# Attention stage turned round: keys on the partitions instead of queries

## The reference, cut to what matters

```python
# 8 heads, q: 1024 queries of 96 numbers, k: 1280 keys (1024 + 256), v: 64 numbers a key
def one(qi):                                   # a block of 128 queries
    s = einsum('bqhd,bkhd->bhqk', qi, k) * 96 ** -0.5
    p = softmax(s, axis=-1)                    # over the 1280 keys
    return einsum('bhqk,bkhd->bqhd', p, v)
...
yd = attn * silu(d_gate)                       # then into the output product
```

## Time and profile before

| what | value |
|---|---|
| runs, median (lowest to highest) | 3601.41 us (3597.78 to 3604.99) |
| the profiled execution's own time | 3603.62 us |
| its span | 3601.8 us |
| busy share of the span: PE, PEld | 91%, 84% |
| DVE, ACT, POOL | 56%, 26%, 6% |
| attention loop in the span | from 3015.8 to 3414.0 us |

### The profile page before, as it was taken

One profiled execution on the slowest core, in us unless ns is written; L12 is line 12 of the kernel. 1 busy time (PEld: TensorE's weight loads), 2 busy tenths in 40 slices (PEclk: granted clock), 3 DMA queues, 4 the chain that ended last, 5 costly groups with the idle time before them and its releaser, 6 DMA issues. The chain is left out here.

```text
span 3601.8 us, 47693 instructions
## 1 busy us (share of the span) xinstructions
PE 3289.2 (91%) x20158; PEld 3042.2 (84%) x20158; DVE 2008.2 (56%) x2814; ACT 943.8 (26%) x1178; POOL 227.4 (6%) x224
## 2 busy tenths in 40 slices
PE   3999999999688779999999999899988996988887
PEld 3999999999677679999999999899988983555465
DVE  5565655566568444566446446645445535666446
ACT  3222222222323331121111111221133314444323
POOL 0000000000005200000000000000012000222200
PEclk9999999999798789999999999999989997999898
DMA  3222222222343344321321321411121321000031
GB/s 100 91 78 75 90 85 86 90 89 74 137 102 50 95 170 135 129 77 53 106 81 46 108 79 38 153 37 43 50 74 37 128 87 74 1 1 1 22 133 69
DMA packets 102463, 285.76 MB, mean 79 GB/s; under 512 B 13157, under 2 KB 32101, under 8 KB 101993
## 3 DMA queue, kind: packets, MB, share of 16 engines
q1 hardware_dynamic: 102248, 282.70, 24.6%
HBM read 218.68 MB, written 63.98 MB: 78 GB/s over the span
## 5 line engine op out<-in xcount | busy, mean ns | idle before, releaser
L491 PE MATMUL mixer_in_dense<-mix_z_high,mixer_in_whigh 128*128 128x348 f32 x1344 | 445.8, 332 | 11.3 <-POOL mixer_in_out L328 11.3
L491 PE MATMUL mixer_in_dense<-mix_z_high,mixer_in_wlow 128*128 128x348 f32 x1344 | 439.1, 327 | 0.0
L491 PE MATMUL mixer_in_dense<-mix_z_low,mixer_in_whigh 128*128 128x348 f32 x1344 | 438.2, 326 | 0.0
L1372 PE MATMUL flow_dense<-rst_norms_operand_b_high,flow_whigh 128*128 128x342 f32 x1248 | 399.2, 320 | 0.4 <-DVE flow_wlow L1464 0.4
L1372 PE MATMUL flow_dense<-irst_norms_operand_b_low,flow_whigh 128*128 128x342 f32 x1248 | 398.3, 319 | 0.0
L1372 PE MATMUL flow_dense<-rst_norms_operand_b_high,flow_wlow 128*128 128x342 f32 x1248 | 397.4, 318 | 0.0
L1930 PE MATMUL joint_dense<-rst_norms_operand_b_high,joint_whigh 128*128 128x342 f32 (+2 forms) x1056 | 344.7, 326 | 17.0 <-DVEq L2047 10.1
L1930 PE MATMUL joint_dense<-rst_norms_operand_b_high,joint_wlow 128*128 128x342 f32 (+2 forms) x1056 | 341.7, 324 | 0.0
L1930 PE MATMUL joint_dense<-irst_norms_operand_b_low,joint_whigh 128*128 128x342 f32 (+2 forms) x1056 | 340.6, 323 | 0.0
L1372 PE MATMUL flow_dense<-first_operand_a_high,flow_whigh 128*128 128x342 f32 (+1 forms) x912 | 291.4, 320 | 26.9 <-DVEq L1485 26.9
L1372 PE MATMUL flow_dense<-first_operand_a_low,flow_whigh 128*128 128x342 f32 (+1 forms) x912 | 291.8, 320 | 0.0
(11 more groups left out here) (544 smaller groups left out, 6201.3 us busy)
## 6 DMA issues: line engine op xcount, KB each, us to landing
mixer_in_wstage<-w_in SPq DMA_DIRECT2D x56, 512.0 KB, 4.6
mixer_in_mod_w<-w_mod SPq DMA_DIRECT2D x64, 384.0 KB, 3.6
first_norms_weights<-w_up SPq DMA_DIRECT2D x44, 512.0 KB, 3.5
flow_side<-h SPq DMA_DIRECT2D x24, 512.0 KB, 4.3
h<-flow_out SPq DMA_DIRECT2D x24, 512.0 KB, 3.2
first_norms_weights<-ab_w_in SPq DMA_DIRECT2D x20, 512.0 KB, 3.6
p<-mixer_in_out SPq DMA_DIRECT2D x16, 528.0 KB, 2.9
first_norms_weights<-w_down SPq DMA_DIRECT2D x16, 512.0 KB, 3.5
```

Source lines behind the costliest of these rows:

```text
L491: mm = pe.matmul(pd[s % 2][:, 0:W], a[n % 2][:, P * m:P * (m + 1)], z[x][:, m, W * b:W * (b + 1)], start=m == 0 and i == 0, stop=m == DT - ...
L1372: mm = pe.matmul(o, w[n % NW][:, P * k:P * (k + 1)], x[h][:, k, where], start=k == 0 and e == 0, stop=k == kt - 1 and e == 2)
```

## The change

Each half of a head (512 queries) becomes one unit, 16 in all, with the keys on the partitions:

- `peak`: for each of four tiles of 128 queries one pass of high*high over the 1280 keys, into 3 PSUM banks (one buffer); DVE `largest` takes the maxima. These belong to the next unit.
- `rows`: PE turns the four columns of maxima into a row of 512, negated (product with -identity), ACT `row` copies it as a 97th row of the queries; the keys get a 97th row of ones. So the score product itself subtracts the maximum.
- `chunk`: ten times the whole product for 128 keys x 512 queries (three matmuls of 512 columns) into a ring of three PSUM banks; ACT takes exp of it straight into the buffer from which `value_sums` reads. No transposes, no moves.
- sums over keys: POOL `add_keys` adds the ten blocks (5 blocks to 5, then 2 to 2, 1 to 1, 1 to 1), PE `key_sums` multiplies with ones, DVE `finish` takes 1/sum of 64 x 512, multiplies it with the gate, adds the two halves of the values product, and multiplies.
- For the last unit DVE does `add_keys`.

The order within a unit is written out in `unit`; DVE's program for unit U begins with `finish(U-2)`.

```diff
+    def made_at(U):
+        h, b = divmod(U, 2)
+        if h + 1 >= NH:
+            return (), (), ()
+        if b:
+            return (), (("q", h + 1, 1),), ()
+        return (("k", h + 1, 0),), (("k", h + 1, 1), ("k", h + 1, 2)), (("q", h + 1, 0),)
+
+    def unit(U):
+        own = [[("e", U, k)] for k in range(NKT)]
+        first_, second_, third_ = made_at(U)
+        if U == 0:
+            for k in range(NKT):
+                own[k].append(("v", k))
+        if U + 1 < UNITS:
+            for q, k in enumerate((1, 3, 5, 7)):
+                own[k].append(("peak", U + 1, q))
+            own[6].append(("rows", U + 1, 0))
+        if U:
+            for p, k in enumerate((2, 3, 5, 7)):
+                own[k].append(("sums", U - 1, p))
+        own[2] += first_
+        own[4] += second_
+        own[8] += third_
+        if U + 1 < UNITS:
+            own[9].append(("rows", U + 1, 1))
+        if U:
+            own[9] += [("keys", U - 1), ("sums", U - 1, 4)]
+        return [n for k in own for n in k]
...
+        def add_keys(ch, tt, U):
+            p = PT[U % 2]
+            ch.do(tt(acc[:, :, :], p[:, 0:5, :], p[:, 5:10, :], ALU.add))
+            ch.do(tt(acc[:, 0:2, :], acc[:, 0:2, :], acc[:, 2:4, :], ALU.add))
+            ch.do(tt(acc[:, 0, :], acc[:, 0, :], acc[:, 1, :], ALU.add))
+            ch.do(tt(acc[:, 0, :], acc[:, 0, :], acc[:, 4, :], ALU.add))
...
+                def peak(U, q):
...
+                    if i:
+                        pe.wait_ge(maxed, i)
+                    q0 = HALF * b + P * q
+                    for k0, w in ((0, 512), (512, 512), (1024, 256)):
+                        mm = pe.matmul(pS[:, k0:k0 + w], qh[h % 2][0:KD, q0:q0 + P], kh[h % 2][0:KD, k0:k0 + w],
+                                       start=True, stop=True, skip_group_check=True)
+                    mm.then_inc(peaked, 1)
+
+                def rows(U, r):
...
+                    for q in (2 * r, 2 * r + 1):
+                        i = 4 * U + q
+                        pe.wait_ge(maxed, i + 1)
+                        mm = pe.matmul(pR[:, P * q:P * q + P], mx[:, i:i + 1], minus[:, :], start=True, stop=True,
                                        skip_group_check=True)
...
+                def chunk(n):
...
+                    if k == 0:
+                        pe.wait_ge(lows, HL.at(h, f"rope{b}"))
...
+                        pe.wait_ge(rows_in, U + 1)
                     o = wait_free(pe, n)
+                    pe.matmul(o, kh[j][0:KD + 1, keys], qh[j][0:KD + 1, at], start=True, stop=False)
+                    pe.matmul(o, kl[j][0:KD, keys], qh[j][0:KD, at], start=False, stop=False)
+                    pe.matmul(o, kh[j][0:KD, keys], ql[j][0:KD, at], start=False, stop=True).then_inc(full, 1)
+
+                def value_sums(U, p):
+                    h = U // 2
+                    if p == 0:
+                        if U == 0:
+                            pe.wait_ge(v_made, 1)
+                        else:
+                            pe.wait_ge(y_added, U)
+                        pe.wait_ge(exped, NKT * (U + 1))
...
+                def key_sums(U):
+                    pe.wait_ge(added, U + 1)
+                    if U:
+                        pe.wait_ge(inverted, U)
+                    pe.matmul(pK, c["ones"][:, 0:VD], acc[:, 0, :], start=True, stop=True).then_inc(keys_full, 1)
...
+                def row(U):
+                    act.wait_ge(rows_full, U + 1)
+                    act.activation(qh[U // 2 % 2][KD:KD + 1, half_of(U)], pR, ACT.Copy).then_inc(rows_in, 1)
...
+                            act.activation(PT[U % 2][:, k, :], pt[ring[n] % RING], ACT.Exp, scale=scale).then_inc(exped, 1)
...
+                def largest(U, q):
+                    i = 4 * U + q
+                    dve.wait_ge(peaked, i + 1)
+                    dve.tensor_reduce(mx[:, i:i + 1], pS[:, 0:T2], AX.X, ALU.max).then_inc(maxed, 1)
+
+                def finish(U):
+                    h, at, own = U // 2, half_of(U), rows_of(U)
+                    dve.wait_ge(keys_full, U + 1)
+                    ch.do(dve.reciprocal(ri[own, :], pK))
+                    dve.sem_inc(inverted, 1)
+                    if U == 0:
+                        dve.wait_ge(gates_in, 64)
+                    ch.inc(tt(ri[own, :], ri[own, :], dg[own, h // 2, at], ALU.mult))
+                    dve.wait_ge(y_moved, U + 1)
+                    if h >= 2:
+                        dve.wait_ge(y_low, 2 * (h // 2 - 1) + U % 2 + 1)
+                    ch.do(tt(yp[own, at], pY[own, :], ytmp[own, :], ALU.add))
+                    dve.sem_inc(y_added, 1)
+                    ch.do(tt(yp[own, at], yp[own, at], ri[own, :], ALU.mult))
+                    dve.sem_inc(y_ready, 1)
...
+                ch = Chain(pool, pstep)
+                for U in range(UNITS - 1):
+                    pool.wait_ge(exped, NKT * (U + 1))
+                    if U:
+                        pool.wait_ge(keys_full, U)
+                    add_keys(ch, pool.tensor_tensor, U)
+                    pool.sem_inc(added, 1)
```

More of the change, by code:

```diff
@@ L2399, in attend @@
+    first = tuple(("k", 0, b) for b in range(3)) + tuple(("q", 0, b) for b in range(2))
+    program = [unit(U) for U in range(UNITS)]
+    names = first + tuple(n for own in program for n in own if n[0] in "ekqv")
+    ring = Places(names)
+    by_act = ring.count([n for n in names if n[0] == "v" and n[1] % 2 == 0])
+    by_dve = ring.count([n for n in names if n[0] in "kqv" and n not in by_act])
     with Phase(nc, "attn") as ph:
@@ L2490, in pair_scores @@
[L2490 to L2499, removed]
-                    o = wait_free(pe, n)
[L2501 to L2527, removed]
+                            pe.wait_ge(ones_in, 2)
@@ L2541, in _ @@
                     make(n)
[L2542 to L2547, removed]
-                            make(n)
[L2549 to L2558, removed]
+                for q in range(4):
+                    peak(0, q)
@@ new lines, in _ @@
+                rows(0, 0)
+                rows(0, 1)
+                for U in range(UNITS):
+                    for n in program[U]:
+                        if n[0] == "e":
+                            chunk(n)
+                        elif n[0] == "peak":
+                            peak(n[1], n[2])
+                        elif n[0] == "rows":
+                            rows(n[1], n[2])
+                        elif n[0] == "sums":
+                            value_sums(n[1], n[2])
+                        elif n[0] == "keys":
+                            key_sums(n[1])
+                        else:
+                            make(n)
@@ L2560, in _ @@
+                for p in range(4):
+                    value_sums(UNITS - 1, p)
+                key_sums(UNITS - 1)
+                value_sums(UNITS - 1, 4)
             @block.scalar
             def _(act):
[L2562 to L2573, removed]
@@ new lines, in _ @@
+                dve.wait_ge(step, ch.n)
+                for q in range(4):
+                    largest(0, q)
+                for U in range(UNITS + 2):
+                    if U == UNITS:
+                        dve.wait_ge(exped, NKT * UNITS)
+                        dve.wait_ge(keys_full, UNITS - 1)
+                        add_keys(ch, tt, UNITS - 1)
+                        dve.sem_inc(added, 1)
+                    if U >= 2:
+                        finish(U - 2)
+                    if U >= UNITS:
+                        y_rest(U - 2)
+                        continue
+                    for n in program[U]:
+                        if n[0] == "peak":
+                            largest(n[1], n[2])
+                            if n[2] == 2 and U >= 2:
+                                y_rest(U - 2)
+                        elif n[0] == "v":
+                            if n not in by_act:
+                                dve.wait_ge(full, ring[n] + 1)
+                                dve.tensor_copy(V[:, n[1], :], pt[ring[n] % RING]).then_inc(dve_freed, 1)
+                                if n[1] == NKT - 1:
+                                    dve.wait_ge(act_freed, by_act[("v", NKT - 2)])
+                                    dve.wait_ge(dve_freed, by_dve[n])
+                                    dve.sem_inc(v_made, 1)
+                        elif n[0] in "kq":
+                            low(n)
+                    if U == UNITS - 1:
+                        y_rest(U - 2)
```

236 lines of the change are left out of this document (92 added, 144 removed).

## The result

The changed kernel took 3675.87 us (median of 4 runs, 3672.19 to 3678.55); the kernel before, run beside it, 3599.6. The ratio is 1.0216, interval 1.0203 to 1.0229: slower by some 76 us, where 3592 was forecast and 3632 was the end of the range. The profiled execution took 3672.19 us with a span of 3670.0. Every median here is over undisturbed executions: one of the kernel before, beside the last two experiments, took 4802 us at a clock of 0.64 and is left out.

A forecast was written before the change was run, and what follows sets the result against it. The prediction took the loop as bound by its chain of waits, not one engine. The ends' -26.8 us plus 17.6 for the clock gave -9.2: 3592 against the median 3601.4 (3594 for the profiled execution); range 3560 to 3632.

The forecast's parts named there:

- what PE needs: PE's work: 15.2 of 22.84 us per half head in the old loop, 13.7 us per unit after the change.
- The walk: Step-by-step timing of DVE, PE and ACT through one unit from chunk 0: periods 22.9 and 22.3, mean 22.6 us.
- the hold: In `finish`, POOL's first and second additions delay DVE's two-SBUF-input products: gate product done at 5.75, last product at 8.7 us.
- The reciprocal is hidden: In `finish`, DVE's 3.34 us reciprocal runs beside POOL's first addition; up to 5.3 us for it costs nothing.
- The clock's term: Granted clock falls in most units' thin PE stretch: 1.2 us a unit, 15.6 for 13 units, plus 2 in the tail.
- the signs that the prediction named: Reciprocals 3.3 us, products far over 0.69, PE's wait about 3.9 us, period 22.6 to 24, clock near 0.85, among others.
- The ends: Start, first and last units and tail: the stage ends at 3387.2 instead of 3414.0 without the clock, 26.8 us less.
- Rival 5: Loop: more small waits missing from the walk, 2 us a unit and up, with the clock; 3640 and above; chance 0.05.
- Rival 2: Loop: PE stays at 1.2 GHz through second and third peak of every unit, 3 us x 13; 3616; chance 0.27.
- Rival 3: `finish`: DVE and POOL do not hold each other, saving 38 us and 15 of clock cost; 3540; chance 0.06.

The follow-up runs named there:

- reordered kernel: Changed kernel with DVE doing halves' sum, first maximum, reciprocal, second and third maximum, then the two products; ACT's upper-half copy moved from exponential 5 to 8: 3576.77 us.
- experiment 3: Changed kernel with 14 small float32 matmuls as fillers, results unread, put on PE just before its wait for `y_added`: 3659.42 us, ratio 1.0167.
- the eighth experiment: Reordered kernel with reciprocal and both products together right after the first maximum, and ACT's copy back at exponential 5: 3624.72 us, ratio 1.0091.
- experiment 4: Changed kernel with four of the ten values products of a unit left out, one from each of four pairs: 3673.57 us, ratio 1.0205.

## Why the prediction was wrong

**The step that failed: what PE needs.** "A pair of values products 0.43 (four take 1.08, two at a time); a float32 matmul of 512 columns 0.43 (eight take 3.70)". The counts are of records, two to a float32 matmul: four are one pair, 1.0 us, and eight in 3.70 are four matmuls (their records start 0.43 apart, 3218.70 to 3220.41), 0.86 us each. (The Trainium skill, "FP8 and Floating Point Precision", "TensorE Precision Notes", says that true FP32 takes 4 passes through the array. The trace agrees: four times the 0.23 us of one score matmul is 0.92, near the 0.86 to 1.0 measured.) The sum for a unit then is 13.7 + 5 x 0.57 for the pairs + 1.1 for q and k (1.31 for half of q and half of k's 0.95 + 1.43, 2.5 against 1.4) + 0.43 for the key sum = 18.1. `rows` takes 2 x 0.53 for 0.45, and some seven chunks and four peaks 0.1 to 0.2 more next to float32 work: about 2 more, 20. The reordered kernel shows 20.6.

I had a check and talked it away. The earlier trace rows had PE busy for 271.80 of 300 us, 20.7 of 22.84 a half head, and the prediction said that it "overstates" this, as matmuls overlap. It hardly did. By it PE had 2 us of slack in a period, not 7.6; and the change's work, as the reordered kernel does it, is 20.6. The change takes **nothing** off PE: the transposes that go are paid for by peaks and rows.

**What followed.** The walk was right to the first maximum and wrong behind it. From chunk 0 of the unit above at 3213.71:
- `y_added` at 6.3 (6.5 forecast), PE's stall 3.45 (3.85), last product done 8.4 (8.7), first maximum done 10.05 (10.25). Gate product and last product took 2.52 and 2.01 here (2.43 and 1.80 in the mean), as the hold asked.
- second maximum done at 13.07 (12.45 forecast), q full at 16.2 (13.0), third maximum done 21.6 (18.4), fourth 24.0 (20.65), end of the unit 27.4 (22.3). The 3.2 us that come in by q are the pair, q's own matmuls and a chunk, dearer than thought and in part at 0.50; the last 1.8 are a `rows`, a pair and the key sum.

In other words, with 20.6 us of work, PE can afford neither a stall nor a low clock. By the window of the changed kernel PE is idle for (300 - 253.18) / 300 x 28.6 = 4.5 us of a unit and busy for 24.1, of which 20.6 is the work as the reordered kernel does it at a clock of 0.99; the other 3.5 come with the clock at 0.87. That is 20.6 + 4.5 + 3.5 = 28.6, where the forecast had 13.7 of work and waits of DVE and PE on each other to fill up to 22.6, and 1.2 for the clock. "The reciprocal is hidden" was true of `y_added` and false of the unit.

**Right:** reciprocal 3.35 us (3.34), POOL's first addition 5.69 (5.8), exponential 0.60, row 0.59, the hold and its size, clock 0.87 ("near 0.85"). The clock's term of 1.2 us a unit is the other one that was short: experiment 3 gave 1.1 back, but PE's work grows by 3.5 us a unit with the low clock, and between the two odd units nearly all of such a growth reached the time. Of the signs that the prediction named, stalls, held products and clock came and the period alone did not: none of the others measured PE's work.

**The ends.** Units 0 and 1 and the tail have the same dear float32 work; how their 16 and 14 us divide was not tested. In the tail the last values products wait for the last sum and then run at the low clock:

```profile
3468.19 6.14 PE L2554 MATMUL attn_banks<-attn_probs,attn_values 128*64 128x512 f32 x16 [9.96 <-DVEq L2724]
```

Four pairs, 6.14 us, where 1.7 had been reckoned; the clock is 0.50 from 3468 to 3472.

**The rivals.** Rival 5, "more of them, 2 us a unit and up, with the clock" at 3640 and above, is what happened, at a chance of 0.05. It should have been a rival with a mechanism: that PE's busy time is as it reads. It was at hand: 271.80 against 15.2 x 300 / 22.84 = 200 is a gap of 72 us that needed an explanation by rows. Rival 2 had the right sign and its mechanism is in the trace: the second peak of the unit above runs at half clock, and its 3 us a unit are near the 3.5 that PE's work grows by. But it stood on the same 13.7 us of work, and at 3616 it too is 60 us short. Rival 3 had the hold at 38 and 15 us (64 measured), on a base that was too low.

**What stays open.** How much of the 3.5 us that the low clock adds to PE's work in a unit reaches the end was not separated: the fillers gave back 1.1 with the clock still at 0.95, while 1.57 of the 1.77 by which the busy time of the two odd units differs did reach it. Of the 49 us between the eighth experiment and the sixth, how much is the hold, how much the shorter blocks and how much ACT's copy was not separated either. In the reordered kernel, what would have to go beside PE's work to pass on all of a cut was not tried.

## What to carry to other kernels

Before a busy time is called overstated, make the engine's work add up to it from rows, with the count of records checked against the count of instructions in the code; a gap of a quarter is a finding, not noise. When the largest engine is at nine tenths, judge a change by the stalls it gives that engine, and cut long blocks on the helper engines (here 8 us of DVE) into pieces between the results that it waits for. Order alone was worth 96 us here, more than the change itself moved the time, and it took the contention between DVE and POOL off the path as well.

## What the runs showed of the hardware

- A float32 matmul of 512 columns takes 0.86 to 1.0 us in this kernel and leaves two records, one with fp32r operands 0.23; two float32 products of 64 output partitions each, into the two halves, take 1.0 us together, as one alone does (experiment 4).
- In the unit above, after a stall of 3.45 us, the granted clock still read 1.0 at the stall's end; it was 0.50 from about 0.7 to 7 us behind that end, when PE worked again, and 1.0 after it. In the unit at 3097.45 (stall's end at 3104.18) it was 0.50 from about 0.5 to 10.5 us behind; in the unit after that (3133.18) it fell 1.2 us ahead of the stall's end and rose 5.4 behind. So in these units most of the low clock falls on the work behind a stall.
